# Bias rows made first, stored once, copied 128 times in DRAM and read in shifted rows from ScalarE's queue

## The chip, the cores and the metric

The kernel runs on one core of a Trainium2 chip. A core has TensorE (PE, matmuls into PSUM banks), VectorE (DVE), ScalarE (ACT), GpSimd (POOL) and SyncE (SP), which issues DMAs; ScalarE can issue DMAs from a queue of its own too. 16 DMA engines move the data. The metric is device time in microseconds (us) for one execution, the median of the runs.

## What is computed

Two blocks of two layers each, over 512 tokens of width 1024. The change touches the first block only. There each layer projects the tokens with one wide matrix, runs three attentions and projects back:

```python
def hybrid_layer(x, w_in, w_out, ...):
    h = rms_norm(x, g_pre)
    a_q, a_kv, a_g, b_cq, b_ckv, b_kr, c_q, c_kv, z = split_cols(h @ w_in)
    o_a = nsa_attention(..., rel_bias[:NSA_HEADS])        # 4 heads: compressed, selected, window
    ...
    o_b = causal_block_attention(...)                     # 4 heads, no relative bias
    o_c = banded_attention(..., SWA_WINDOW, rel_bias[NSA_HEADS:], sinks)   # 8 heads, window 128
    mixed = concatenate([o_a, o_b, o_c]) * silu(z)
    return x + rms_norm(mixed @ w_out, g_post)
```

Attentions a and c add to each logit a bias that depends on the head and on the distance of query and key alone: `bias_heads[:, t5_bucket(dist)]`, a table of 32 buckets for each of the 12 heads. In the second block (pooling, a recurrence and two feed-forward layers per layer) nothing changes.

## The kernel before

All weights are streamed from DRAM in tiles of 128 x 1024 (512 KB). `fetch_first` (L338) issues the load of tile n from SyncE into one of four raw buffers. VectorE casts it to a rounded part (`one_hi`, L172) and subtracts to get the rest (`one_lo`, L174), into one of two slots; PE multiplies both with the rounded activations and the rounded part with the rest of the activations, 24 matmuls per tile. A raw buffer is free when its tile is split (`w_split`), so SyncE's program in `attend` is a row of waits and fetches, tile n after the split of tile n - 4.

The first layer's 24 input tiles run in order 0 to 23. Tiles 0 and 1 are multiplied together while x arrives (`rows_arriving`, L219 to L222), later ones by `weight_tile` (L449, L453, L456). After tile 3 PE sums the squares of x (L1048); ScalarE then makes 1/rms by Ln and Exp (L702, L705), and only then VectorE evicts the finished banks into `proj` (L789, L791). Six banks are free at the start, so tile 6 is the first that needs an eviction, and VectorE's program evicts tiles 0 to 3 before it casts the tile 6. At tile 10 VectorE uses `s1`, a set of small weights (L875, `nsink`); after tile 18 PE uses `w1`. ScalarE issues both loads (L699, L700) after its passes over x. Behind the input tiles come 48 attention pairs, in the order NSA (24 pairs, tiles 0 and 1 of the output), MLA (8), sliding window (16).

The relative bias is made on the chip. `distance_rows` multiplies the table `rel` (32 x 12) with a one-hot matrix `hot` of the distances (L559: 4 heads x 1024 distances in two matmuls, L562: 8 heads x 384), `mask_rows` adds a mask (L569, L572), and the result is `vec` on partitions 0 to 3 and `near` on partitions 0 to 7. For the attention, row p of a bias tile must be the head's row shifted by p. This is done through DRAM: `store_bias` writes each head's row 128 times (`far_bias` 4 x 128 x 1024, 2.10 MB; `near_bias` 8 x 128 x 384, 1.57 MB), and `read_bias` reads with a partition step one element shorter than the row, into `biasA` and `biasC`.

In this order: PE does `distance_rows` between tile 1 and tile 2 (it waits for five small loads, `k1` among them, which SyncE issues after x and two weight tiles); VectorE does `mask_rows` at i = 1; SyncE does `store_bias` after fetching tile 7 and `read_bias` after fetching tile 11. VectorE waits for `read_a` and `read_c` before the first attention pair and before the first sliding-window pair.

Of the kernel before, what the change touches and what calls it, by code (L numbers as in the profile page):

```python
# [27 lines left out]
P = 128  # L28
# [348 lines left out]
TURN_LAG, WEIGH_LAG = 3, 4  # L377
N_NSA, N_MLA = 24, 8
SPLIT_AT = (17, 20)
# [4 lines left out]
Y_BANKS = (0, 4, 1, 2, 6, 7, 3, 5)  # L384
XSUM_BANK = 3
Y_KEPT = 2

# [72 lines left out]
class First:  # L460


    def __init__(self, kit, ctx):
# [19 lines left out]
        with ExitStack() as early:  # L483
# [20 lines left out]
        self.start = kit.sems("start", ("gains_in", "x_in0", "x_in1", "x_in2", "x_in3", "loaded", "vec_mm", "vec_made",  # L504
                                        "stored", "read_a", "read_c", "set"))
        self.s = [kit.sems(f"first{l}", FIRST_SEMS) for l in range(DEPTH)]
# [3 lines left out]
def start_engines(kit, first):  # L510

    d, bank, st, s = kit.d, kit.bank, kit.stream, first.start

    def sync(sp):
        sp.dma_start(kit.gains[:], d["gains"]).then_inc(s["gains_in"], 16)
        for i in range(4):
            sp.dma_start(kit.x[:, 2 * i:2 * i + 2, :], d["x"][:, 2 * i:2 * i + 2, :]).then_inc(s[f"x_in{i}"], 16)
            if i < 2:
                fetch_first(sp, st, i)
        for dst, src in ((first.rel, "rel"), (first.hot, "hot"), (first.msk, "msk"), (first.msk_near, "msk_near"),  # L520
                         (kit.k1, "k1")):
# [24 lines left out]
    def vector(v):  # L546
        v.sem_inc(st.w_split, RAW_RING)
        v.memset(kit.eps[:, 0:1], NORM_EPS).then_inc(s["set"], 1)
        v.memset(kit.eps[:, 1:2], LN_EPS / ALPHA ** 2).then_inc(s["set"], 1)
        v.memset(kit.ones[:], 1.0).then_inc(s["set"], 1)  # L550

    def tensor(pe):
        pe.sem_inc(st.mm_done, HL_RING)
        pe.wait_ge(s["set"], 3)

    def distance_rows(pe):
        pe.wait_ge(s["loaded"], 80)
        for i in range(2):
            pe.matmul(bank[(5, 3)[i]][0:A_HEADS, :], first.rel[:, 0:A_HEADS], first.hot[:, i * T:(i + 1) * T],  # L559
                      start=True, stop=True).then_inc(s["vec_mm"], 1)  # L560
        pe.wait_ge(s["vec_made"], 1)
        pe.matmul(bank[5][0:C_HEADS, 0:NEAR_W], first.rel[:, A_HEADS:], first.hot[:, 256:256 + NEAR_W],  # L562
                  start=True, stop=True).then_inc(s["vec_mm"], 1)

    def mask_rows(v):
        v.wait_ge(s["loaded"], 80)
# [5 lines left out]
        v.tensor_tensor(first.near[:], bank[5][0:C_HEADS, 0:NEAR_W], first.msk_near[:], ALU.add  # L572
                        ).then_inc(s["vec_made"], 1)

    return dict(sync=sync, store_bias=store_bias, read_bias=read_bias, scalar=scalar, vector=vector, tensor=tensor,
                distance_rows=distance_rows, mask_rows=mask_rows)


def attend(kit, first, l, begin):
# [26 lines left out]
    turn_bank = [(3, 6)[g % 2] for g in range(len(groups))]  # L606
    out_bank = {t: (4, 7)[i % 2] for i, t in enumerate(TILES)}

# [70 lines left out]
    def sync(sp):  # L679
        for n in range(max(n0, RAW_RING), n0 + st.per_layer):  # L680
            sp.wait_ge(st.w_split, n + 1)
            fetch_first(sp, st, n)
            if n == 7:
                begin["store_bias"](sp)
            if n == 11:
                begin["read_bias"](sp)

    def scalar(a):
# [63 lines left out]

        convert_at = {NU - 4: (0, 1), NU - 3: (2, 3), NU - 2: (4,), NU: (5,), NU + 1: (6,)}
        for j in range(NU + TURN_LAG):
            for i in here(j):
                u = pairs[i]
                w = u["width"]
                if u["kind"] == "swa":
                    a.wait_ge(s["sinks_in"], i + 1 - N_NSA - N_MLA)
                    w += 1  # L760
# [5 lines left out]
            for x in here(j - TURN_LAG):  # L766
                for g in groups_of[x]:
                    if not copied_by_v[g]:
# [4 lines left out]
                        a.activation(dst, src, ACT.Copy).then_inc(s["pt_by_a"], 1)  # L773
            for p in convert_at.get(j, ()):
                convert(p)
        convert(DC - 1)

    def vector(v):
# [27 lines left out]
        def step(j):  # L806
            for x in here(j - WEIGH_LAG - 1):
                if x == NU - 1 or pairs[x + 1]["tile"] != pairs[x]["tile"]:
                    tile = pairs[x]["tile"]
                    v.wait_ge(s["pv_mm"], x + 1)  # L810
# [46 lines left out]
        for i in range(N_IN):  # L857
            if i < N_IN - HL_RING:
                split(i + HL_RING)
            if i == 1:  # L860
                if l == 0:
                    begin["mask_rows"](v)
                for c in range(1, DC):
# [9 lines left out]
            if i == 10:  # L873
# [5 lines left out]
                if l == 0:  # L879
                    v.wait_ge(start["stored"], 32)  # L880
                v.tensor_tensor(rot_k[:, 0, :], proj[64:96, C_KR, :], cos, ALU.mult).then_inc(s["rot_made"], 1)
                v.tensor_tensor(rot_k[:, 1, :], proj[96:128, C_KR, :], sin, ALU.mult).then_inc(s["rot_made"], 1)
# [51 lines left out]
        v.wait_ge(s["z_made"], DC)  # L934
        v.wait_ge(start["read_a"], 16)
        for j in range(NU + WEIGH_LAG + 1):
            if j == N_NSA + N_MLA:
                v.wait_ge(start["read_c"], 16)
# [4 lines left out]
    def tensor(pe):  # L943
# [33 lines left out]
        def weigh(x):  # L977
# [3 lines left out]
            wait_copies(pe, groups_of[x][-1])  # L981
            order = TILES.index(tile)
            if order >= 2:
                pe.wait_ge(s["mixed"], order - 1)
            for y in range(u["m"]):
# [6 lines left out]
        def step(j):  # L992
            for i in here(j):
                if i >= 2:
                    pe.wait_ge(s["logits"], 2 * (i - 1))
                if i == 0:
                    pe.wait_ge(s["kc_made"], 2)
                if i == N_NSA:
                    pe.wait_ge(s["qk_made"], 2 * B_HEADS)
                    pe.wait_ge(s["uk_kept"], B_HEADS)  # L1000
                for hh in range(2):
                    logits(i, hh)
# [26 lines left out]
        if before:  # L1029
# [3 lines left out]
                      lambda k: pe.wait_ge(s["xhi_made"], k + 1), lambda k: pe.wait_ge(s["xlo_made"], k + 1))  # L1033
        if l == 0:
            begin["distance_rows"](pe)
        for i in range(2, N_IN):
# [5 lines left out]
            if i == 3:  # L1042
                if l == 0:
                    pe.wait_ge(start["vec_made"], 3)
                if before:
# [3 lines left out]
                          ).then_inc(s["xsq_summed"], 1)  # L1049
            if i == 12:  # L1050
                pe.wait_ge(s["taken"], C_KR + 1)
                for n in range(NT):
# [61 lines left out]
    def gpsimd(g):  # L1114
# [4 lines left out]
        for i in range(NU):  # L1119
            g.wait_ge(s["inv_made"], i + 1)  # L1120
            if i == 0:
                g.wait_ge(s["gates"], 4)
# [1339 lines left out]
```

## Time and profile before

| | us |
|---|---|
| median of 3 runs (lowest to highest) | 2673.74 (2669.78 to 2679.16) |
| profiled execution | 2676.89 |
| its span, first to last instruction | 2674.8 |
| busy in it: PE / DVE / ACT / POOL | 2472.3 / 1294.3 / 661.5 / 654.8 |
| mean granted TensorE clock | 0.962 |

The profile is one execution. A timeline row gives the start, the time taken, the engine (SPq and ACTq are DMA issues), the line, output and input, and in brackets the idle time before it and what ended that. Neighbours of one kind are merged into a row with their count. A row of windows gives busy times in a stretch, the granted clock (1.00 is full), the share of 16 DMA engines that was busy and the rate. Wait rows name who waited for whom.

### The profile page before, as it was taken

The page shows a single profiled execution, that of the slowest core. Times are in us where ns is not written, and L with a number is a line of the kernel's source. Part 1 is how long each engine was busy: PE and PEld are TensorE (multiplying, and loading weights), DVE is VectorE, ACT ScalarE, POOL GpSimd, SP SyncE. Part 2 cuts the span into 40 slices and gives each one's busy share as a digit, 9 for nine tenths or more (in the row PEclk, how much of TensorE's full clock was granted, in tenths as well). Part 3 has the DMA queues.
Part 4 walks back from the last instruction along what each step waited for, and adds up shares of the span by engine and source line. Part 5 has one row for each costly group of instructions (what it writes and reads, how often), then busy time and mean ns, then how long its engine had stood idle before and what let it go on. Part 6 is the DMA issues. An engine that isn't in the chain of part 4 may idle for free. (4 is left out here: it accounts for less than half of the span.)

```text
span 2674.8 us, 35071 instructions
## 1 busy us (share of the span) xinstructions
PE 2472.3 (92%) x13238; PEld 1985.8 (74%) x13238; DVE 1294.3 (48%) x1920; ACT 661.5 (25%) x1329; POOL 654.8 (24%) x510
## 2 busy tenths in 40 slices
PE   7089999999789999999899999899999998999997
PEld 5066677866668888788688888788888787788886
DVE  4045656557453334586643334433343776533344
ACT  3001643037121110253321110311100643311101
POOL 1000561016333331200333321233311101433311
PEclk9589999999989999998999999999999998999999
DMA  5341013200033332221223232223322221223322
GB/s 166 56 139 47 17 48 126 86 25 17 16 117 98 98 109 93 71 98 41 79 87 101 94 117 92 64 94 98 107 98 83 95 65 56 79 95 101 111 99 78
DMA packets 58641, 224.79 MB, mean 84 GB/s; under 512 B 6392, under 2 KB 8576, under 8 KB 58276
## 3 DMA queue, kind: packets, MB, share of 16 engines
q1 hardware_dynamic: 57380, 215.49, 25.3%
q10 hardware_dynamic: 1152, 7.78, 0.8%
q8 instruction: 77, 1.26, 0.2%
q14 instruction: 32, 0.26, 0.0%
HBM read 217.47 MB, written 5.77 MB: 83 GB/s over the span
## 5 line engine op out<-in xcount | busy, mean ns | idle before, releaser
L172 DVE CAST two_hi<-two_raw 128x1024 fp32r<-128x1024 f32 (+1 forms) x292 | 219.8, 753 | 908.0 <-PE bank L241 896.5
L234 PE MATMUL bank<-xh,two_hi 128*128 128x512 f32 x1728 | 429.6, 391 | 0.0
L241 PE MATMUL bank<-xl,two_hi 128*128 128x512 f32 x1728 | 427.5, 389 | 0.0
L237 PE MATMUL bank<-xh,two_lo 128*128 128x512 f32 x1728 | 426.9, 389 | 0.0
L174 DVE TENSOR_TENSOR two_lo<-two_raw,two_hi 128x1024 fp32r<-128x1024 f32 (+1 forms) x292 | 401.0, 1373 | 10.0
L237 PEld LDWEIGHTS bank<-xh,two_lo 128*128 128x128 f32 x1728 | 324.3, 188 | 67.5
L241 PEld LDWEIGHTS bank<-xl,two_hi 128*128 128x128 f32 x1728 | 324.3, 188 | 67.4
L234 PEld LDWEIGHTS bank<-xh,two_hi 128*128 128x128 f32 x1728 | 323.0, 188 | 68.2 <-issue 1.1
L1579 POOL TENSOR_TENSOR up_hm<-up_sg,up_hm 128x512 f32<-128x512 f32 x88 | 197.6, 2245 | 556.4 <-ACT up_hm L1561 556.4
L449 PE MATMUL bank<-xh,one_hi 128*128 128x512 f32 x448 | 122.5, 418 | 81.0 <-DVE one_hi L172 81.0
L234 PE MATMUL bank<-hh,two_hi 128*128 128x512 f32 x704 | 171.8, 392 | 0.0
L172 DVE CAST one_hi<-one_raw 128x1024 fp32r<-128x1024 f32 x64 | 45.5, 710 | 260.6 <-PE bank L456 134.8
L241 PE MATMUL bank<-hl,two_hi 128*128 128x512 f32 x704 | 171.4, 390 | 0.0
L237 PE MATMUL bank<-hh,two_lo 128*128 128x512 f32 x704 | 170.0, 389 | 0.0
L449 PEld LDWEIGHTS bank<-xh,one_hi 128*128 128x128 f32 x448 | 88.0, 198 | 104.8 <-issue 86.0
L1561 ACT ACTIVATE up_hm<-bank 128x512 f32<-128x512 f32 x88 | 52.9, 601 | 416.5 <-PE bank L241 413.7
L665 POOL TENSOR_SCALAR lg_ring<-lg_ring,inv,gate 128x31 f32<-128x31 f32 (+4 forms) x80 | 45.0, 570 | 450.6 <-DVE inv L799 450.3
L234 PEld LDWEIGHTS bank<-hh,two_hi 128*128 128x128 f32 x704 | 132.1, 188 | 29.3 <-issue 1.9
L237 PEld LDWEIGHTS bank<-hh,two_lo 128*128 128x128 f32 x704 | 132.1, 188 | 27.5
L241 PEld LDWEIGHTS bank<-hl,two_hi 128*128 128x128 f32 x704 | 132.2, 188 | 27.3
L1582 POOL TENSOR_TENSOR hl<-up_hm,hh 128x512 f32 x88 | 115.1, 1308 | 83.7 <-ACT hh L1563 83.7
L453 PE MATMUL bank<-xh,one_lo 128*128 128x512 f32 x448 | 112.7, 394 | 0.0
(289 smaller groups left out, 2923.2 us busy)
## 6 DMA issues: line engine op xcount, KB each, us to landing
two_raw<-in_up SPq DMA_DIRECT2D x180, 512.0 KB, 3.4
two_raw<-in_down SPq DMA_DIRECT2D x64, 704.0 KB, 4.0
one_raw<-in_w_in SPq DMA_DIRECT2D x48, 512.0 KB, 3.5
two_raw<-in_w_in SPq DMA_DIRECT2D x40, 512.0 KB, 3.4
one_raw<-in_w_out SPq DMA_DIRECT2D x16, 512.0 KB, 3.4
two_raw<-in_w_out SPq DMA_DIRECT2D x16, 512.0 KB, 4.1
w<-in_w ACTq DMA_DIRECT2D x2, 2048.0 KB, 11.6
x<-in_x SPq DMA_DIRECT2D x4, 512.0 KB, 6.9
```

What stands on the lines that cost most here:

```text
L172: v.tensor_copy(st.hi[:, h, 0:w], st.raw[:, r, 0:w]).then_inc(st.hi_made, 1)
L174: v.tensor_tensor(st.lo[:, h, 0:w], st.raw[:, r, 0:w], st.hi[:, h, 0:w].bitcast(F32), ALU.subtract).then_inc(st.w_split, 1)
L234: pe.matmul(out[:], st.hi[:, slot, k * P:(k + 1) * P], xh[:, h * kp + k, :], start=h == 0 and k == 0, stop=False)
L237: pe.matmul(out[:], st.lo[:, slot, k * P:(k + 1) * P], xh[:, h * kp + k, :], start=False, stop=False)
L241: mm = pe.matmul(out[:], st.hi[:, slot, k * P:(k + 1) * P], xl[:, h * kp + k, :], start=False, stop=h == pieces - 1 and k == kp - 1)
L449: pe.matmul(out[:], st.hi[:, slot, w * P:(w + 1) * P], xh[:, k, :], start=k == 0, stop=False)
L453: pe.matmul(out[:], st.lo[:, slot, w * P:(w + 1) * P], xh[:, k, :], start=False, stop=False)
L665: return eng.tensor_scalar(row, row, inv[:, i, hh:hh + 1], gate[:, u["n"], b:b + 1], ALU.mult, ALU.mult)
L1561: a.activation(hm[:, f, :], bank[1][:], ACT.Copy).then_inc(s["out_taken"], 1)
L1579: g.tensor_tensor(hm[:, f, :], sg[:, f, :], hm[:, f, :], ALU.mult).then_inc(s["h_made"], 1)
L1582: g.tensor_tensor(hl[:, at, :].rearrange("p o t -> p (o t)"), hm[:, f, :], hh[:, at, :].rearrange("p o t -> p (o t)").bitcast(F32), ALU.su ...
```

## The change

The row matmuls and the masked adds are done before the first weight tile is split; their inputs `rel`, `hot`, `msk`, `msk_near` are loaded first, and the near matmul uses bank 7, so that it need not wait for bank 5. SyncE stores the rows once (`far_row`, `near_row`, 28 KB). ScalarE copies them 128 times from DRAM to DRAM behind its passes over x, ahead of the loads of s1 and w1, and issues the shifted reads after the last of its eight Silu passes, behind a wait for the copies. `k1` has its own semaphore and is loaded after the row stores. Some constants of the attention's order are written as expressions.

```diff
     def sync(sp):
+        for dst, src in ((first.rel, "rel"), (first.hot, "hot"), (first.msk, "msk"), (first.msk_near, "msk_near")):
+            sp.dma_start(dst[:], d[src]).then_inc(s["loaded"], 16)
         sp.dma_start(kit.gains[:], d["gains"]).then_inc(s["gains_in"], 16)
         for i in range(4):
             sp.dma_start(kit.x[:, 2 * i:2 * i + 2, :], d["x"][:, 2 * i:2 * i + 2, :]).then_inc(s[f"x_in{i}"], 16)
             if i < 2:
                 fetch_first(sp, st, i)
-        for dst, src in ((first.rel, "rel"), (first.hot, "hot"), (first.msk, "msk"), (first.msk_near, "msk_near"),
-                         (kit.k1, "k1")):
-            sp.dma_start(dst[:], d[src]).then_inc(s["loaded"], 16)
         for n in (2, 3):
             fetch_first(sp, st, n)
-
-    def store_bias(sp):
         sp.wait_ge(s["vec_made"], 3)
-        sp.dma_start(d["far"], first.vec[0:A_HEADS].unsqueeze(1).to_broadcast([A_HEADS, P, 2 * T])
-                     ).then_inc(s["stored"], 16)
-        sp.dma_start(d["near"], first.near[:].unsqueeze(1).to_broadcast([C_HEADS, P, NEAR_W])).then_inc(s["stored"], 16)
-
-    def read_bias(sp):
-
-        sp.wait_ge(s["stored"], 32)
-        for dst, name, sem, heads, w, n in ((kit.biasC, "near", "read_c", C_HEADS, NEAR_W, 256),
-                                            (kit.biasA, "far", "read_a", A_HEADS, 2 * T, BIAS_W)):
+        sp.dma_start(d["far_row"], first.vec[:]).then_inc(s["stored"], 16)
+        sp.dma_start(d["near_row"], first.near[:]).then_inc(s["stored"], 16)
+        sp.dma_start(kit.k1[:], d["k1"]).then_inc(s["k1_in"], 16)
+
+    spread = (("near", "read_c", kit.biasC, C_HEADS, NEAR_W, 256), ("far", "read_a", kit.biasA, A_HEADS, 2 * T, BIAS_W))
+
+    def copy_bias(a):
+
+        a.wait_ge(s["stored"], 32)
+        for name, _, _, heads, w, _ in spread:
+            row = d[f"{name}_row"]
+            a.dma_start(d[name], bass.AP(row.tensor, row.offset, [[w, heads], [0, P], [1, w]])).then_inc(s["copied"], 16)
+
+    def read_bias(a):
+
+        a.wait_ge(s["copied"], 32)
+        for name, sem, dst, heads, w, n in spread:
             src = d[name]
-            sp.dma_start(dst[:], bass.AP(src.tensor, src.offset + P - 1, [[w - 1, P], [w * P, heads], [1, n]])
-                         ).then_inc(s[sem], 16)
+            a.dma_start(dst[:], bass.AP(src.tensor, src.offset + P - 1, [[w - 1, P], [w * P, heads], [1, n]])
+                        ).then_inc(s[sem], 16)
...
         v.memset(kit.ones[:], 1.0).then_inc(s["set"], 1)
+        mask_rows(v)
 
     def tensor(pe):
         pe.sem_inc(st.mm_done, HL_RING)
         pe.wait_ge(s["set"], 3)
-
-    def distance_rows(pe):
-        pe.wait_ge(s["loaded"], 80)
+        pe.wait_ge(s["loaded"], 64)
         for i in range(2):
             pe.matmul(bank[(5, 3)[i]][0:A_HEADS, :], first.rel[:, 0:A_HEADS], first.hot[:, i * T:(i + 1) * T],
                       start=True, stop=True).then_inc(s["vec_mm"], 1)
-        pe.wait_ge(s["vec_made"], 1)
-        pe.matmul(bank[5][0:C_HEADS, 0:NEAR_W], first.rel[:, A_HEADS:], first.hot[:, 256:256 + NEAR_W],
+        pe.matmul(bank[7][0:C_HEADS, 0:NEAR_W], first.rel[:, A_HEADS:], first.hot[:, 256:256 + NEAR_W],
                   start=True, stop=True).then_inc(s["vec_mm"], 1)
...
             fetch_first(sp, st, n)
-            if n == 7:
-                begin["store_bias"](sp)
-            if n == 11:
-                begin["read_bias"](sp)
...
             a.activation(xsq[:, c, :], kit.x[:, c, :], ACT.Square).then_inc(s["xsq_made"], 1)
+        if l == 0:
+            begin["copy_bias"](a)
         a.dma_start(s1[:], d["s1"][l]).then_inc(s["s1_in"], 16)
         a.dma_start(w1[:], d["w1"][l]).then_inc(s["w1_in"], 16)
...
             a.activation(proj[:, C_Z + c, :], proj[:, C_Z + c, :], ACT.Silu).then_inc(s["z_made"], 1)
+            if l == 0 and c == DC - 1:
+                begin["read_bias"](a)
...
-        convert_at = {NU - 4: (0, 1), NU - 3: (2, 3), NU - 2: (4,), NU: (5,), NU + 1: (6,)}
+        convert_at = {}
+        for p in range(DC - 1):
+            at = max(NU - L_RING + p // 2 + TURN_LAG + 1, last_of[TILES[p]] + WEIGH_LAG + 2, *convert_at)
+            convert_at.setdefault(at, []).append(p)
...
+    for kind, heads, w in (("far", A_HEADS, 2 * T), ("near", C_HEADS, NEAR_W)):
+        dram[f"{kind}_row"] = nc.dram_tensor(f"{kind}_bias_row", (heads, w), F32, kind="Internal").ap()
```

## Rows read from the trace of the kernel before

**Rows 1.** The page's slices: busy tenths of PE and of the DMA engines.
```profile
PE   7089999999789999999899999899999998999997
...
DMA  5341013200033332221223232223322221223322
```
**Rows 2.** Waits from 0 to 160 us: who waited for whom, us in total, times, longest.
```profile
DVE one_hi L172 <- DMA one_raw<-in_w_in: 93.8, 2, 88.4
...
PE bank L449 <- DVE one_hi L172: 81.0, 1, 81.0
```
**Rows 3.** Timeline of SyncE's DMA issues around the stores and reads of the bias.
```profile
30.82 34.25 SPq L530 DMA_DIRECT2D near_bias<-near  x1
...
65.11 56.72 SPq L345 DMA_DIRECT2D one_raw<-in_w_in  x1
...
143.66 0.39 SPq L538 DMA_DIRECT2D biasC<-near_bias  x1
```
**Rows 4.** Timeline of PE: first matmuls of tile 7, tile 8, tile 9 and tile 10.
```profile
59.18 1.98 PE L449 MATMUL bank<-xh,one_hi 128*128 128x512 f32 x8
...
145.76 3.75 PE L449 MATMUL bank<-xh,one_hi 128*128 128x512 f32 x8 [80.98 <-DVE one_hi L172]
...
153.09 1.98 PE L449 MATMUL bank<-xh,one_hi 128*128 128x512 f32 x8
...
158.53 1.98 PE L449 MATMUL bank<-xh,one_hi 128*128 128x512 f32 x8
```
**Rows 5.** Windows; the last three columns are granted clock, DMA share and GB/s.
```profile
17.50:20.00 2.50, 2.50 (x13) 2.06 (x12) 0.00 (x0) 2.46 (x5) 2.09 (x2) 1.00 1.02 415
...
30.00:33.00 3.00, 3.00 (x9) 2.38 (x8) 2.64 (x4) 0.00 (x0) 0.00 (x0) 0.52 0.48 157
...
36.00:64.00 28.00, 28.00 (x123) 22.79 (x123) 11.37 (x14) 6.06 (x9) 0.00 (x0) 1.00 0.24 26
66.00:96.00 30.00, 0.00 (x0) 0.00 (x0) 0.00 (x0) 0.00 (x0) 0.00 (x0) 0.53 0.46 51
```
**Rows 6.** Timeline of PE and DVE: row matmuls, masked adds, tile 2, start of tile 3.
```profile
25.53 1.88 PE L559 MATMUL bank<-hot,rel 32*4 32x512 f32 x4
...
27.85 1.27 DVE L569 TENSOR_TENSOR vec<-bank,msk 4x512 f32<-4x512 f32 x2
...
28.58 0.81 PE L562 MATMUL bank<-hot,rel 32*8 32x384 f32 x2 [1.18 <-DVE vec L569]
29.31 3.14 PE L449 MATMUL bank<-xh,one_hi 128*128 128x512 f32 x8
...
36.51 1.98 PE L449 MATMUL bank<-xh,one_hi 128*128 128x512 f32 x8
```
**Rows 7.** Timeline of the start: issues of x, rel and k1, first cast, PE's run.
```profile
1.22 0.41 SPq L517 DMA_DIRECT2D x<-in_x  x1
...
4.33 0.74 SPq L522 DMA_DIRECT2D rel<-in_rel  x1
...
5.49 0.72 ACT L695 ACTIVATE xh<-x,gains 128x512 fp32r<-128x512 f32 x1 [3.46 <-DMA x<-in_x]
...
6.41 0.36 SPq L522 DMA_DIRECT2D k<-in_k  x1
6.67 0.69 DVE L172 CAST one_hi<-one_raw 128x1024 fp32r<-128x1024 f32 x1 [5.49 <-DMA one_raw<-in_w_in]
...
13.51 0.80 PE L219 MATMUL bank<-xh,one_hi 128*128 128x512 f32 x1 [2.66 <-DVE one_lo L174]
```
**Rows 8.** Timeline: the norm's Ln on ScalarE, and VectorE's first use of s1.
```profile
43.01 0.69 ACT L702 ACTIVATE xrstd<-bank,eps 128x512 f32<-128x512 f32 x1 [23.05 <-PE bank L1048]
...
166.72 0.16 DVE L875 TENSOR_SCALAR nsink<-s 128x8 f32<-128x8 f32 x1
```
**Rows 9.** Timeline: one conversion of xh; and a window inside the last stores, columns as in 5.
```profile
360.71 0.62 ACT L751 ACTIVATE xh<-proj 128x512 fp32r<-128x512 f32 x1
...
2666.50:2668.00 1.50, 0.00 (x0) 0.00 (x0) 1.46 (x3) 0.72 (x1) 0.00 (x0) 0.50 0.69 281
```

More of the change, by code:

```diff
@@ L385 @@
 XSUM_BANK = 3
+OUT_BANKS = (4, 7, 4, 7, 4, 7, 4, 7)
 Y_KEPT = 2
@@ L504, in __init__ @@
         self.start = kit.sems("start", ("gains_in", "x_in0", "x_in1", "x_in2", "x_in3", "loaded", "vec_mm", "vec_made",
-                                        "stored", "read_a", "read_c", "set"))
+                                        "k1_in", "stored", "copied", "read_a", "read_c", "set"))
         self.s = [kit.sems(f"first{l}", FIRST_SEMS) for l in range(DEPTH)]
@@ L571, in mask_rows @@
         v.wait_ge(s["vec_mm"], 3)
-        v.tensor_tensor(first.near[:], bank[5][0:C_HEADS, 0:NEAR_W], first.msk_near[:], ALU.add
+        v.tensor_tensor(first.near[:], bank[7][0:C_HEADS, 0:NEAR_W], first.msk_near[:], ALU.add
                         ).then_inc(s["vec_made"], 1)
-    return dict(sync=sync, store_bias=store_bias, read_bias=read_bias, scalar=scalar, vector=vector, tensor=tensor,
-                distance_rows=distance_rows, mask_rows=mask_rows)
+    return dict(sync=sync, copy_bias=copy_bias, read_bias=read_bias, scalar=scalar, vector=vector, tensor=tensor)
 def attend(kit, first, l, begin):
@@ L606, in attend @@
     turn_bank = [(3, 6)[g % 2] for g in range(len(groups))]
-    out_bank = {t: (4, 7)[i % 2] for i, t in enumerate(TILES)}
+    out_bank = {t: OUT_BANKS[i] for i, t in enumerate(TILES)}
+    last_of = {u["tile"]: i for i, u in enumerate(pairs)}
+    first_of = {kind: min(i for i, u in enumerate(pairs) if u["kind"] == kind) for kind in ("cmp", "mla", "swa")}
+    n_swa = [sum(u["kind"] == "swa" for u in pairs[:i + 1]) for i in range(NU)]
+    assert list(TILES) == sorted(TILES, key=last_of.get)
     def here(j):
@@ L758, in scalar @@
                 if u["kind"] == "swa":
-                    a.wait_ge(s["sinks_in"], i + 1 - N_NSA - N_MLA)
+                    a.wait_ge(s["sinks_in"], n_swa[i])
                     w += 1
@@ L773, in scalar @@
                         a.activation(dst, src, ACT.Copy).then_inc(s["pt_by_a"], 1)
-            for p in convert_at.get(j, ()):
+            for p in convert_at.pop(j, ()):
+                convert(p)
+        for late in convert_at.values():
+            for p in late:
                 convert(p)
@@ L807, in step @@
             for x in here(j - WEIGH_LAG - 1):
-                if x == NU - 1 or pairs[x + 1]["tile"] != pairs[x]["tile"]:
-                    tile = pairs[x]["tile"]
+                tile = pairs[x]["tile"]
+                if x == last_of[tile]:
                     v.wait_ge(s["pv_mm"], x + 1)
@@ L860, in vector @@
             if i == 1:
-                if l == 0:
-                    begin["mask_rows"](v)
                 for c in range(1, DC):
@@ L880, in vector @@
                     v.wait_ge(start["stored"], 32)
+                    v.wait_ge(start["k1_in"], 16)
                 v.tensor_tensor(rot_k[:, 0, :], proj[64:96, C_KR, :], cos, ALU.mult).then_inc(s["rot_made"], 1)
@@ L934, in vector @@
         v.wait_ge(s["z_made"], DC)
-        v.wait_ge(start["read_a"], 16)
         for j in range(NU + WEIGH_LAG + 1):
-            if j == N_NSA + N_MLA:
+            if j == first_of["cmp"]:
+                v.wait_ge(start["read_a"], 16)
+            if j == first_of["swa"]:
                 v.wait_ge(start["read_c"], 16)
@@ L981, in weigh @@
             wait_copies(pe, groups_of[x][-1])
-            order = TILES.index(tile)
-            if order >= 2:
-                pe.wait_ge(s["mixed"], order - 1)
+            ahead = [p for p in range(TILES.index(tile)) if OUT_BANKS[p] == out_bank[tile]]
+            if ahead:
+                pe.wait_ge(s["mixed"], ahead[-1] + 1)
             for y in range(u["m"]):
@@ L995, in step @@
                     pe.wait_ge(s["logits"], 2 * (i - 1))
-                if i == 0:
-                    pe.wait_ge(s["kc_made"], 2)
-                if i == N_NSA:
+                if i == first_of["mla"]:
                     pe.wait_ge(s["qk_made"], 2 * B_HEADS)
                     pe.wait_ge(s["uk_kept"], B_HEADS)
+                if i == first_of["cmp"]:
+                    pe.wait_ge(s["kc_made"], 2)
                 for hh in range(2):
@@ L1033, in tensor @@
                       lambda k: pe.wait_ge(s["xhi_made"], k + 1), lambda k: pe.wait_ge(s["xlo_made"], k + 1))
-        if l == 0:
-            begin["distance_rows"](pe)
         for i in range(2, N_IN):
@@ L1050, in tensor @@
             if i == 12:
+                if l == 0:
+                    pe.wait_ge(start["k1_in"], 16)
                 pe.wait_ge(s["taken"], C_KR + 1)
@@ L1120, in gpsimd @@
             g.wait_ge(s["inv_made"], i + 1)
-            if i == 0:
+            if i == first_of["cmp"]:
                 g.wait_ge(s["gates"], 4)
```

3 lines of the change are left out of this document (1 added, 2 removed).

## The prediction

> **What bounds the kernel now.** I read the slices of the page first: TensorE (PE) is busy in nine tenths or more of nearly every slice, except the second, where it does nothing, and the DMA line falls to 1 to 3 tenths around it [rows 1]. The kernel is bound by TensorE, so the second slice (67 to 134 us) is pure loss. The list of waits names it: PE waits 81.0 us once for the first cast (L172) of a weight tile, and that cast waits 88.4 us for its DMA [rows 2]. The timeline of SyncE's queue says why. The near store's issue, right behind the far one's, begins at 30.82 and takes 34.25 us, and the next weight fetch's issue takes 56.72 us; the reads of the bias follow at 143.66, when the near store has landed [rows 3]. PE ran to 64.8 us on the eight weight tiles fetched ahead of the stores, and started tile 8 at 145.76 [rows 4].
>
> How fast the stores go is in the windows. While only the far store moves (36 to 64 us) the DMA share is 0.24, which is four of 16 engines, at 26 GB/s in all; from 66 to 96 us it is 0.46 at 51 GB/s, twice each. When ordinary loads run, 16 engines move 415 GB/s, 26 GB/s each [rows 5]. So one DMA engine carries one head's copies, and four engines that read partitions 0 to 3 together get what one engine gets in a load: 6.5 GB/s each. The far store alone (2.10 MB) needs 81 us at 26 GB/s; near heads 0 to 3 wait behind it on the same engines. All weight fetches use all 16 engines in queue order, so they wait too. The Trainium skill gives the rule for it ("SBUF — State Buffer", Door 1: The DMA port swizzle): partitions 0 to 3 share one of 16 ports. The trace agrees, with its 26 GB/s for four engines and 51 for eight.
>
> **The change, part by part.** All terms are against the profiled execution, 2676.9 us (span 2674.8).
>
> 1. The hole. The bulk copies leave SyncE's queue, whose stores are now 28 KB instead of 3.67 MB. Weight fetches then find their queue free, as between tiles 2 and 7. A tile takes 5.44 us on PE (158.53 less 153.09), so tile 9 would begin at 59.18 + 10.88 = 70.1 where it began at 153.09 [rows 4]: 83.0 us. That is the wait of 81.0 plus 1.9 us by which tile 8 ran long (7.33 us). The granted clock had fallen to 0.50 while PE idled [rows 5]. What is late next is worked out in 4 and 5.
>
> 2. The row matmuls. Before, they stood between tiles 1 and 2: PE began them at 25.53, began tile 2 at 29.31, and tile 2 took until 36.51, 7.20 us in place of 5.44, with the granted clock at 0.52 from 30 to 33 us [rows 6, 5]. Without them tile 2 follows at once: 3.8 + 1.7 = 5.5 us gained.
>
> 3. The start. SyncE now issues four small loads ahead of the gains and x: 6.41 less 4.33 = 2.1 us of issue, by which x and weight tile 0 (cast at 6.67) come later, about 8.8 [rows 7]. VectorE (DVE) now does the three masked adds (two take 1.27 us, [rows 6]) before its first split, and waits for PE's row matmuls. The loads are issued by 2.8 us and the first of the kind needs about 2 us to land, an estimate from x, which ACT could use 4.3 us after its issue with half a megabyte in it. Then 4.8 us; the far matmuls take 1.9 us at full clock, perhaps 3.5 on a cold one; a third of 0.8 to 1.3, a last add: 9 to 10.5 us. So the splits begin 2.1 to 3.8 us later than at 6.67 and with them PE's run from 13.51. I take 3.7, near the upper end, since PE has not run by then: lost. Terms 2 and 3 give -1.8. SyncE itself waits in front of the row stores until 10.5, and behind them are k1 and fetch 4. Fetch 4 needs the first split (about 14 us now), so nothing waits for that.
>
> 4. ScalarE's queue. The two copies are issued there, behind a wait for the row stores (they queue behind about 4.3 MB of loads at 0.4 MB/us, so they land at about 17 to 18; copies flow from 19). Behind that wait stand s1, w1, and then Ln and Exp of the norm, without which DVE can evict nothing. An issue can block: the near store's returned when 34 of the far store's 81 us were gone [rows 3], that is with some 75 of 128 pieces left on each engine. So the issue of s1 returns when the last 60% of the far copy remain. The Ln began at 43.01 [rows 8], now 41.2. DVE's order puts four evictions (2.5 us) and the cast of tile 6 (0.7) behind Ln and Exp (1.4), and PE wants tile 6 at 59.18 - 5.44 - 1.8 = 51.9: ScalarE may be late until 47.3 without loss.
> What does a copy from DRAM to DRAM cost? No row shows one. From below: an engine reads DRAM at 26 GB/s [rows 5] and writes DRAM at 25.5 (the last stores, 281 GB/s on a share of 0.69, [rows 9]). If both sides overlap it is 0.16 us for 4 KB; if they follow each other, 12.8 GB/s and 0.32 us. From above: 6.5 GB/s as in the old store, though here no SBUF partition is read. Far has 128 pieces of 4 KB on each of 4 engines, near 128 of 1.5 KB on each of 8 (taking the same split by heads). Overlapped: near 7.7, far 20.5 us. Serial: near 15.4, far 41 us; s1's issue returns after 15.4 + 0.41 x 41 = 32 us, at 51, and at 59 if the fetches of 5 to 9 and k1 (8 us on each engine) fit into no gap. Late by 4 to 12 us; I take serial, and 8 us: the engine reads and writes the same memory, and a source row of 4 KB is read 128 times over. The Trainium skill ("DMA: Bandwidth & Descriptors", Latency and other measured facts) has 207 to 214 GB/s each way for copies between HBM tensors, 13 GB/s an engine; by it the sum would be the serial one. No run here shows it yet.
>
> 5. s1, w1 and the reads. s1 is needed at 166.72 [rows 8], now 82 (90 with the 8 us of term 4). The far copy ends at 19 + 56 = 75, at most 92 with all fetches serial; s1 lands some 3 us later. Covered or nearly: up to 5 us in the range. w1 is needed by PE after tile 18, past 120. The reads of biasC and biasA hold ScalarE until the copies are done; behind it is work of tile 12 and later (from about 90), and biasA is wanted only when the attention begins, past 170. Nothing.
>
> 6. The rest of the diff writes constants as expressions of the pair list. With this order the values are the same, but for one: converting p = 5 (0.62 us, [rows 9]) comes two pairs earlier, in both layers. 0, between -0.6 and +0.6 each.
>
> Sum: -83.0 - 1.8 + 8 = -76.8, so 2600 us against the profiled 2676.9. The median of the runs is 3.1 us under that execution: 2597.
>
> The rule of the skill that speaks against the change is in the same page ("DMA: Bandwidth & Descriptors", Issuing engines are not separate DMA queues): work issued by ScalarE runs on the same 16 DMA engines, so that another queue only saves issue time. The trace before shows only one queue busy in the hole. By that rule the transfer itself gains nothing from the move; my gain comes from order within a queue and from the source.
>
> **The rivals.**
> A. Copies overlap, 26 GB/s an engine: s1's issue returns at 19 + 16 + 8 = 43, before 47.3. No stall: 2676.9 - 84.8 = 2592, median 2589. For it: both sides alone run at that speed. Against it: one row read over and over, and reads and writes in one memory.
> B. The copy is as slow as the store was, 6.5 GB/s an engine: near 30, far 81 us; s1's issue returns at 19 + 30 + 33 = 82, late by 35; s1 lands at about 138, where 82 + 35 = 117 was wanted, 20 more: -85 + 55, 2647, median 2644. This is also the case in which the change doesn't do what it says. For it: the same piece sizes and four engines. Against: eight engines gave 51 GB/s on other partitions, so partitions, not pieces, set the pace.
> C. Slower than before: the copy from DRAM doesn't split by heads but goes on one engine. 3.67 MB at 26 GB/s is 141 us, s1's issue returns at about 19 + 60 + 70 = 149, late by 102 against 84.8 gained: +17, 2694, median 2691; at the serial price +150. At the serial price it decides below three engines. For it: no row shows a split of a copy without partitions; against: its outer dimension is the heads as before.
> D. One descriptor generator serves both queues, so SyncE's fetches 6 and 7 (at 30 us) wait behind the copies until 51 to 59. Tile 6 then begins at about 60 instead of 51.9, beside the stall of term 4 and not on top: 2 us more than the forecast. It lies within it.
>
> **How the numbers follow.** Serial copies (with D) 0.47; A 0.30; between serial and B, or B itself, 0.17; C 0.03; others, mostly a few us of the start, 0.03. The forecast is 2597. Bounds: 2583 (A with a start that costs 2 and not 3.7, and a few us of unseen gain) to 2628 (an engine at about 8 GB/s: near 25, far 66, s1's issue back at 71, late by 24, and s1 then some 6 late). That leaves out B proper and C. Under 0.3% (8 us) this kernel's runs can't tell from no change. Faster 0.95, same 0.01, slower 0.04 (C, and something like it).
>
> **What would show it.** No wait of cast L172 on its DMA over 5 us, PE in the second slice at 9 tenths, tile 2 right behind tile 1 at full clock; DMA share near 0.25 to 0.5 at 50 to 200 GB/s beside the fetches from 19 us on; the issue of s1 on ScalarE's queue some 30 to 40 us long and Ln at 50 to 58 instead of 41. If Ln is at 41, A was right; if DVE waits at nsink for s1, B. Wrong altogether if the fetches of SyncE wait on the shared DMA engines behind the copies, tile after tile, longer than 5.44 us each: that would be a new hole between 50 and 90 us.

## The result and the profile after

| | before | after |
|---|---|---|
| median of 4 runs (lowest to highest), us | 2676.45 (2669.78 to 2680.52) | 2591.00 (2590.79 to 2591.41) |
| profiled execution / its span, us | 2676.89 / 2674.8 | 2590.79 / 2588.9 |
| mean granted clock | 0.962 | 0.977 |

The ratio is 0.9683, 95% interval 0.9661 to 0.9705: 3.2% faster, some 85 us. The forecast was 2597, the range 2583 to 2628. (The kernel before has one run more here than ahead of the prediction, where its median was 2673.74.)

The page's slices of the changed kernel, the rows that answer to [rows 1]. The second slice is full now:

```profile
PE   8999999998799999998999999999999999999997
...
DMA  6300132000333322211223332222321312222332
```

The waits from 0 to 100 us. The 88 us of [rows 2] are gone. What VectorE's cast waits for is PE: 12.2 us once, for tiles 0 and 1, and after that pieces of at most 3.5 us, as it should be where PE is the bound:

```profile
DVE one_hi L172 <- PE bank L456: 25.6, 10, 3.5
ACT xrstd L706 <- PE bank L1058: 20.3, 1, 20.3
```

The timeline of the changed kernel in order of time, from several engines: masked adds and the first cast, PE's run, the copies on ScalarE's queue, tiles 2 and 3, a fetch of SyncE, the issues of s1 and w1, and the norm's Ln (compare [rows 3, 6, 7, 8]).

```profile
6.14 0.68 DVE L572 TENSOR_TENSOR vec<-bank,msk 4x512 f32<-4x512 f32 x1 [4.97 <-PE bank L563]
...
9.53 0.67 DVE L172 CAST one_hi<-one_raw 128x1024 fp32r<-128x1024 f32 x1
...
16.36 0.80 PE L219 MATMUL bank<-xh,one_hi 128*128 128x512 f32 x1 [2.67 <-DVE one_lo L174]
16.44 1.24 ACTq L536 DMA_DIRECT2D near_bias<-near_bias_row  x1
...
17.72 4.94 ACTq L536 DMA_DIRECT2D far_bias<-far_bias_row  x1
...
22.69 16.18 ACTq L703 DMA_DIRECT2D s<-in_s  x1
...
29.80 1.98 PE L449 MATMUL bank<-xh,one_hi 128*128 128x512 f32 x8
...
30.46 0.33 SPq L345 DMA_DIRECT2D one_raw<-in_w_in  x1
...
35.24 1.98 PE L449 MATMUL bank<-xh,one_hi 128*128 128x512 f32 x8
...
38.90 1.21 ACTq L704 DMA_DIRECT2D w<-in_w  x1
41.74 0.69 ACT L706 ACTIVATE xrstd<-bank,eps 128x512 f32<-128x512 f32 x1 [20.33 <-PE bank L1058]
```

In this execution Ln waits for PE and for nothing else. PE runs without a wait from 16.4 to 100 us; tile 9 begins here, where [rows 4] have 153.09:

```profile
68.78 1.98 PE L449 MATMUL bank<-xh,one_hi 128*128 128x512 f32 x8
```

And the windows, with the columns of [rows 5] (the last three: granted clock, DMA share, GB/s). From 20 to 27 us the near copy moves on half of the engines, at 28 us the far one on a quarter, and at 36 us four engines are shared about evenly by the two queues, the far copy on ScalarE's (13.4% of the 16 engines' time) and weight fetches on SyncE's (12.6%):

```profile
20.00:27.00 7.00, 7.00 (x27) 5.67 (x26) 0.00 (x0) 1.40 (x3) 1.18 (x1) 1.00 0.53 199
28.00:30.00 2.00, 2.00 (x10) 1.68 (x9) 1.49 (x2) 0.00 (x0) 0.00 (x0) 1.00 0.26 105
36.00:38.00 2.00, 2.00 (x11) 1.65 (x10) 1.79 (x4) 0.00 (x0) 0.00 (x0) 1.00 0.26 107
```

That is 24 to 26 GB/s for each engine, four times the pace of the old store (0.24 and 26 GB/s in [rows 5]), on the same number of engines.

### The profile page after: what moved, and what is told of

It reads as the page before. It is cut to its first block and busy times, and to the rows that moved or that the text cites. A ratio compares the mean times of both kernels' runs of the same rounds, so it can differ in the third digit from the quotient of the medians.

```text
span 2588.9 us, 35076 instructions
## 1 busy us (share of the span) xinstructions
PE 2472.0 (95%) x13238; PEld 1983.8 (77%) x13238; DVE 1294.7 (50%) x1920; ACT 662.0 (26%) x1329; POOL 655.2 (25%) x510
## 5 line engine op out<-in xcount | busy, mean ns | idle before, releaser
L449 PE MATMUL bank<-xh,one_hi 128*128 128x512 f32 x448 | 116.0, 401 | 0.0
L1575 ACT ACTIVATE hh<-up_hm 128x512 f32 x88 | 55.6, 632 | 215.9 <-POOL up_hm L1591 215.9
```

The source lines that it names most:

```text
L449: pe.matmul(out[:], st.hi[:, slot, w * P:(w + 1) * P], xh[:, k, :], start=k == 0, stop=False)
L1575: a.activation(hh[:, bass.ds(j * 2 + f, 1), :].rearrange("p o t -> p (o t)"), hm[:, f, :], ACT.Copy).then_inc(s["hhi_made"], 1)
```

## The experiments

All times are medians. The changed kernel was timed twice more beside the later ones: 2589.83 (2587.74 to 2595.11) and 2590.98 (2587.30 to 2595.25), where its first four runs lay within 0.6. So kernels of about 2590 have a spread of some 8 us within their runs, and differences of 2 or 3 us between two of them aren't decided by the times.

### What made the old store slow: source or queue

Four corners were wanted: SBUF or DRAM as the source, SyncE's or ScalarE's queue. Two are the kernels before and after, which differ in more than that: the rows are made first in the one after. The third is the changed kernel, reading SBUF from ScalarE's queue:

```diff
-        for name, _, _, heads, w, _ in spread:
-            row = d[f"{name}_row"]
-            a.dma_start(d[name], bass.AP(row.tensor, row.offset, [[w, heads], [0, P], [1, w]])).then_inc(s["copied"], 16)
+        for name, src, heads, w in (("near", first.near, C_HEADS, NEAR_W), ("far", first.vec, A_HEADS, 2 * T)):
+            a.dma_start(d[name], src[0:heads].unsqueeze(1).to_broadcast([heads, P, w])).then_inc(s["copied"], 16)
```

> The changed kernel, but ScalarE's two bulk transfers read the rows from SBUF (128 times each, as the kernel before did) and not from DRAM. Theory SOURCE (the SBUF partitions read set the pace, 6.5 GB/s an engine): the near transfer takes about 31 us, the far one 81; s1's issue returns at about 81 us instead of 38.9, so Ln begins at 82, 35 us later than PE can bear, and s1 lands at about 133 where 117 would be wanted: 2591 + 35 + 16 = 2642 us, up to 2660 if the weight fetches crawl on the shared engines 0 to 3. Theory QUEUE (the gain came from taking the bulk off SyncE's queue): within 10 us of 2591.

Measured: 2644.75 us (2641.47 to 2647.18), ratio 0.9884 (0.9860 to 0.9908). Its timeline of ScalarE and its queue:

```profile
18.00 9.78 ACTq L535 DMA_DIRECT2D far_bias<-vec  x1
27.82 55.91 ACTq L702 DMA_DIRECT2D s<-in_s  x1
83.76 4.96 ACTq L703 DMA_DIRECT2D w<-in_w  x1
88.77 0.69 ACT L705 ACTIVATE xrstd<-bank,eps 128x512 f32<-128x512 f32 x1 [67.11 <-issue]
```

PE's wait in the list of waits up to 160 us (sum, count, longest):

```profile
PE bank L449 <- DVE one_hi L172: 49.3, 3, 41.0
```

The last of its three pieces in the timeline, with what VectorE waited for just before:

```profile
137.71 0.17 DVE L884 TENSOR_SCALAR nsink<-s 128x8 f32<-128x8 f32 x1 [7.31 <-DMA s<-in_s]
...
142.71 3.75 PE L449 MATMUL bank<-xh,one_hi 128*128 128x512 f32 x8 [7.95 <-DVE one_hi L172]
```

And a window, with the columns of [rows 5]:

```profile
64.00:70.00 6.00, 0.00 (x0) 0.00 (x0) 0.00 (x0) 0.00 (x0) 0.00 (x0) 0.50 0.24 25
```

The rate is the old one, 25 GB/s on four engines. ScalarE sat in the issue of s1 for 55.9 us, and PE waited 41.0 us for the evictions behind it. Later it waited 7.95 us for the cast of tile 13, which stands behind `nsink` in VectorE's program, and `nsink` waited for s1. The third piece, 0.4 us, is the only one that a weight tile's fetch caused. This is rival B, and its time (2644) fits in part by luck: it had 35 us for Ln and 20 for s1, where 41.0, 8.0 and some 4 us at the lower clock were measured (tile 6 took 7.26 us instead of 5.44, tile 13 8.18 instead of 5.60). Moving the bulk to the other queue, with the rows made first, saves 35 of 85 us and makes a new wait.

The fourth corner is the kernel before with DRAM as the source, in SyncE's queue at the old place:

```diff
...
-        sp.dma_start(d["far"], first.vec[0:A_HEADS].unsqueeze(1).to_broadcast([A_HEADS, P, 2 * T])
-                     ).then_inc(s["stored"], 16)
-        sp.dma_start(d["near"], first.near[:].unsqueeze(1).to_broadcast([C_HEADS, P, NEAR_W])).then_inc(s["stored"], 16)
+        sp.dma_start(d["far_row"], first.vec[:]).then_inc(s["rows"], 16)
+        sp.dma_start(d["near_row"], first.near[:]).then_inc(s["rows"], 16)
+        sp.wait_ge(s["rows"], 32)
+        for name, heads, w in (("far", A_HEADS, 2 * T), ("near", C_HEADS, NEAR_W)):
+            row = d[f"{name}_row"]
+            sp.dma_start(d[name], bass.AP(row.tensor, row.offset, [[w, heads], [0, P], [1, w]])).then_inc(s["stored"], 16)
```

> The kernel before with one edit: SyncE stores each row once, waits for that, and then copies from DRAM 128 times, all in its own queue at the place of the old store. Theory SOURCE: far 20 us and near 8 us on a few engines from about 33 us, done by about 62, fetch 8 lands by about 64, when PE wants it: no hole, 2676 - 83 = 2593 us (up to 2603). Theory QUEUE: the fetches still stand behind the bulk in one queue, so most of the hole stays: 2650 us or more.

Measured: 2586.07 us (2585.36 to 2591.69), ratio 0.9668 (0.9642 to 0.9694). The queue theory is out. In its trace the far copy runs at 104 GB/s on a share of 0.25, the near store's issue, 34.25 us in [rows 3], takes 7.78:

```profile
33.13 0.72 SPq L533 DMA_DIRECT2D far_bias<-far_bias_row  x1
33.90 7.78 SPq L533 DMA_DIRECT2D near_bias<-near_bias_row  x1
```

Of the hole this is left on PE:

```profile
65.71 2.08 PE L449 MATMUL bank<-xh,one_hi 128*128 128x512 f32 x8 [1.95 <-DVE one_hi L172]
```

So the change of source alone gives the whole gain that the times resolve. It was timed a second time beside the changed kernel:

> The kernel before with the DRAM source alone, copies on SyncE's queue, timed a second time beside the changed kernel. If the source is the whole gain: equal to the changed kernel within 3 us. If the rest of the change (rows first, ScalarE's queue) is worth something by itself, the changed kernel is faster by more than 3 us. From the first time it may be up to 5 us faster than the changed kernel: its PE begins 3 us earlier, pays 3.8 for the row matmuls and 2 for a rest of the hole.

Measured: 2593.62 us (2584.73 to 2595.62) against 2590.98. The two aren't told apart by this; the first time it had stood 5 us below the changed kernel's 2591. Rows made first and the change of queue are worth nothing by themselves that these runs resolve.

### Why that source was slow

The kernel before once more, still from SBUF and from SyncE's queue, with each head's row on a partition of its own four (0, 4, 8 and so on; the tables are made four times as tall, each row four times):

```diff
...
-        sp.dma_start(d["far"], first.vec[0:A_HEADS].unsqueeze(1).to_broadcast([A_HEADS, P, 2 * T])
+        sp.dma_start(d["far"], first.vec[0:4 * A_HEADS:4].unsqueeze(1).to_broadcast([A_HEADS, P, 2 * T])
...
-        sp.dma_start(d["near"], first.near[:].unsqueeze(1).to_broadcast([C_HEADS, P, NEAR_W])).then_inc(s["stored"], 16)
+        sp.dma_start(d["near"], first.near[0:4 * C_HEADS:4].unsqueeze(1).to_broadcast([C_HEADS, P, NEAR_W])).then_inc(s["stored"], 16)
...
-            pe.matmul(bank[(5, 3)[i]][0:A_HEADS, :], first.rel[:, 0:A_HEADS], first.hot[:, i * T:(i + 1) * T],
+            pe.matmul(bank[(5, 3)[i]][0:4 * A_HEADS, :], first.rel[:, 0:4 * A_HEADS], first.hot[:, i * T:(i + 1) * T],
...
```

> The kernel before with one edit: the head rows lie on partitions 0, 4, 8, ... instead of 0, 1, 2, ... (rel, msk, vec and near are four times as tall, each row four times), and the bulk store reads one partition of each four. Still from SBUF, on SyncE's queue, at the old place. If it is the four neighbouring partitions that share 26 GB/s: four engines move about 104 GB/s in the far store, the hole is gone, 2593 us. If a read of one SBUF partition over and over is slow by itself (6.5 GB/s an engine): the hole stays, 2676 us.

Measured: 2588.96 us (2585.41 to 2591.24), ratio 0.9668 (0.9644 to 0.9692). In the window of its far store four engines move 108 GB/s out of SBUF:

```profile
36.00:40.00 4.00, 4.00 (x17) 3.27 (x16) 1.55 (x3) 0.00 (x0) 0.00 (x0) 0.91 0.27 108
```

Reading one partition 128 times isn't slow; four engines reading partitions 0 to 3 are, together. This is the rule of the Trainium skill named in the prediction ("SBUF — State Buffer", Door 1: The DMA port swizzle): partitions 0 to 3 lie behind one port, and 0, 4, 8 and 12 behind four. The trace agrees: 26 GB/s from four partitions of one port, 108 from four ports.

### What a blocked issue costs

The changed kernel with the far copy issued a second time:

```diff
...
+        row = d["far_row"]
+        a.dma_start(d["spare"], bass.AP(row.tensor, row.offset, [[2 * T, A_HEADS], [0, P], [1, 2 * T]])).then_inc(s["copied"], 16)
...
```

> The changed kernel with the far copy issued a second time, into a spare tensor, ahead of s1. It tests the price of a blocked issue and the latest time for Ln. s1's issue should return some 20 us later, at about 59 us, and Ln begin at about 60 instead of 41.7. PE wants tile 6 at 52.5 and Ln must begin by 47.9 for that, so 12.5 us are lost: 2603 us. If the extra copy only uses idle engines and no issue waits for it: 2591 us. If a late s1 or slow fetches count too: above 2610 us.

Measured: 2610.12 us (2607.77 to 2613.10), 19 more than the changed kernel. ScalarE's queue and the first matmuls of tile 6:

```profile
22.36 16.22 ACTq L538 DMA_DIRECT2D spare_bias<-far_bias_row  x1
38.62 22.16 ACTq L705 DMA_DIRECT2D s<-in_s  x1
60.82 1.20 ACTq L706 DMA_DIRECT2D w<-in_w  x1
62.07 0.69 ACT L708 ACTIVATE xrstd<-bank,eps 128x512 f32<-128x512 f32 x1 [40.52 <-issue]
...
66.75 3.75 PE L449 MATMUL bank<-xh,one_hi 128*128 128x512 f32 x8 [15.53 <-DVE one_hi L172]
```

The chain is as worked out: 4.7 us from Ln to the matmuls of tile 6. The further copy held the issue of s1 by its own length, 22 us. PE waited 15.5 and not 12.5: Ln came 2 us later than I had set, and PE was 1.4 us further on in this execution (tile 6 due at 51.05, not 52.46), which adds to the wait and not to the time. The tile after the wait took 7.37 us (66.75 to 74.12) and not 5.44, the granted clock having gone to 0.50: 1.9 us, which I had left out. So tile 7 begins 16.2 us later than in the changed kernel (74.12, there 57.90), of 18.1 by which the two spans differ; another 1.5 are gone by the start of the attention (194.55, there 176.87), at a dip of the clock that comes by chance (see the sum of what was measured, below).

The changed kernel with the rows made late, between tiles 1 and 2 as before, copies on ScalarE's queue:

```diff
-        for dst, src in ((first.rel, "rel"), (first.hot, "hot"), (first.msk, "msk"), (first.msk_near, "msk_near")):
-            sp.dma_start(dst[:], d[src]).then_inc(s["loaded"], 16)
         sp.dma_start(kit.gains[:], d["gains"]).then_inc(s["gains_in"], 16)
...
+            if n == 7:
+                begin["store_rows"](sp)
...
+        if l == 0:
+            begin["distance_rows"](pe)
         for i in range(2, N_IN):
```

> The changed kernel with the first part undone: the four small loads are issued after x, the row matmuls stand between tiles 1 and 2 again and the masked adds behind the fourth split; the copies stay on ScalarE's queue and now start at about 32 us. Theory ISSUE BLOCKS: s1's issue returns 22 us after the copies start, w1's a little later, so Ln begins at about 56 instead of 41.7; PE can bear 48 to 49 here, 7 us are lost, plus 1.3 for the row matmuls' place: 2599 us. Rival (early rows matter only for the row matmuls' place and the clock): 2592 us.

Measured: 2601.01 us (2598.32 to 2605.54), ratio 0.9722 (0.9706 to 0.9738), against 2589.83 for the changed kernel beside it. The intervals lie apart.

```profile
35.65 17.01 ACTq L709 DMA_DIRECT2D s<-in_s  x1
...
53.94 0.69 ACT L712 ACTIVATE xrstd<-bank,eps 128x512 f32<-128x512 f32 x1 [34.19 <-issue]
...
58.62 3.75 PE L449 MATMUL bank<-xh,one_hi 128*128 128x512 f32 x8 [7.49 <-DVE one_hi L172]
```

So making the rows first is not idle: on ScalarE's queue it keeps the issue of s1 from holding Ln. 7.5 us of wait were expected as 7. The tile behind the wait took 8.35 us (58.62 to 66.97) instead of 5.44, so the clock took 2.9 more, which again wasn't in the expectation: 10.4 of the 11.2. It pays for the choice of that queue, no more.

### Can the rest be had

Copies over 16 engines (the 128 repeats outermost in both patterns):

```diff
-            a.dma_start(d[name], bass.AP(row.tensor, row.offset, [[w, heads], [0, P], [1, w]])).then_inc(s["copied"], 16)
+            dst = d[name]
+            a.dma_start(bass.AP(dst.tensor, dst.offset, [[w, P], [P * w, heads], [1, w]]),
+                        bass.AP(row.tensor, row.offset, [[0, P], [w, heads], [1, w]])).then_inc(s["copied"], 16)
```

> The changed kernel with the 128 copies as the outermost dimension of the two copies, so that 16 engines and not 8 and 4 should share each: the DMA share goes to 1.0 at some 400 GB/s from 18 us, all done in about 9 us, s1's issue returns before 30 us. The time stays within 1 us of 2591, since ScalarE was free 5 us before it had to be. If the copies beside the weight fetches cost anything hidden, up to 3 us are gained.

Measured: 2590.01 us (2587.27 to 2598.60). w1's issue is over at 20.9 us instead of 40.1. From 22 to 24 us ScalarE's queue alone moves, nearly all of it the near copy's 1.5 KB pieces:

```profile
22.00:24.00 2.00, 2.00 (x11) 1.65 (x10) 0.00 (x0) 0.00 (x0) 0.00 (x0) 1.00 0.89 307
```

That is 21.5 GB/s an engine, where the same pieces ran at 23.5 on eight engines (199 GB/s on a share of 0.53); in the 2 us behind it the rate was 233 on 0.77, 19. The expectation had some 400 GB/s and all done in 9 us; the far copy landed at 34.9. The time doesn't move: all of it lay beside other work already.

The cheaper start: the small loads from ScalarE's queue, the masked adds behind the first two splits.

```diff
...
     def sync(sp):
-        for dst, src in ((first.rel, "rel"), (first.hot, "hot"), (first.msk, "msk"), (first.msk_near, "msk_near")):
-            sp.dma_start(dst[:], d[src]).then_inc(s["loaded"], 16)
...
     def scalar(a):
+        for dst, src in ((first.rel, "rel"), (first.hot, "hot"), (first.msk, "msk"), (first.msk_near, "msk_near")):
+            a.dma_start(dst[:], d[src]).then_inc(s["loaded"], 16)
...
-        mask_rows(v)
...
             for i in range(HL_RING):
                 split(i)
+            begin["mask_rows"](v)
```

> The changed kernel with a cheaper start: ScalarE issues the four small loads at once, so that SyncE's gains, x and weight tile 0 come as early as in the kernel before, and VectorE splits the first two tiles before the masked adds. PE does the row matmuls in its idle time before tile 0. The run of PE should begin at about 13.5 us instead of 16.4, and the copies at about 18: 2588 us. If the start is not what sets tile 0 (the arrival of x does): 2591 us. If Ln comes too late because the copies start later: above 2591.

Measured: 2590.86 us (2588.00 to 2594.38) against 2589.83. In the trace tile 2 begins at 27.68 where the changed kernel beside it has 29.64, but the changed kernel's own executions differ here (29.80, 29.64, 28.52), and of the 2.0 us 1.7 are lost again at tile 19, which takes 9.1 us here and 7.5 there (127.79 to 136.93, 129.75 to 137.24). The times don't show a gain. PE's run began at 15.09, not 13.5: the first cast was at 8.23, 1.6 later than in [rows 7], probably because the loads from the second queue land among x's; no run shows that apart. This run came nearest to the edge: Ln at 45.01 with the issue of s1 as what held it, and PE wanted it by 45.7 (tile 6 at 50.35, less 4.7).

The 16 engines once more, now in the kernel before with DRAM as the source (SyncE's queue, the old place):

```diff
-            sp.dma_start(d[name], bass.AP(row.tensor, row.offset, [[w, heads], [0, P], [1, w]])).then_inc(s["stored"], 16)
+            dst = d[name]
+            sp.dma_start(bass.AP(dst.tensor, dst.offset, [[w, P], [P * w, heads], [1, w]]),
+                         bass.AP(row.tensor, row.offset, [[0, P], [w, heads], [1, w]])).then_inc(s["stored"], 16)
```

> The same, with the 128 copies outermost, so that 16 engines share them: done in about 9 us at some 400 GB/s, before fetch 8 is issued. The 2 us that PE waited before tile 8 go: 2 us less than the kernel before it in this call, if the spread lets it be seen; in the trace the wait of PE on the cast of tile 8 is gone.

Measured: 2588.25 us (2587.26 to 2593.76) against 2590.98 for the changed kernel and 2593.62 for the same with few engines. There is no wait before tile 8 in the trace, as expected (62.40, 67.84, 73.28: three tiles at 5.44). But there is none either in the trace with few engines beside it (63.33, 68.77, 74.20), where PE was later by itself. What the 16 engines changed is seen on VectorE, at the cast of tile 8, first with few engines, then with 16:

```profile
67.42 0.69 DVE L172 CAST one_hi<-one_raw 128x1024 fp32r<-128x1024 f32 x1 [6.71 <-DMA one_raw<-in_w_in]
...
62.67 0.69 DVE L172 CAST one_hi<-one_raw 128x1024 fp32r<-128x1024 f32 x1 [2.88 <-PE bank L456]
```

The tile had come in time for PE in both; in the first run of the DRAM source it hadn't, by 1.95 us.

And the cheaper start together with copies over 16 engines:

```diff
-            a.dma_start(d[name], bass.AP(row.tensor, row.offset, [[w, heads], [0, P], [1, w]])).then_inc(s["copied"], 16)
+            dst = d[name]
+            a.dma_start(bass.AP(dst.tensor, dst.offset, [[w, P], [P * w, heads], [1, w]]),
+                        bass.AP(row.tensor, row.offset, [[0, P], [w, heads], [1, w]])).then_inc(s["copied"], 16)
...
```

> The changed kernel with the cheaper start (small loads issued by ScalarE, splits ahead of the masked adds) and copies over 16 engines. Tile 2 begins 2 us earlier than in the changed kernel and ScalarE is free by 25 us: 2588 us, 2 less than the changed kernel in this call.

Measured: 2589.98 us (2588.59 to 2590.28); tile 2 begins at 27.48, in the changed kernel beside it at 28.52: 1 us and not the 2 expected. None of these is faster than the changed kernel by more than the spread. From 16.4 us to the attention, at 177, PE waits for 2.7 us in all in the changed kernel; the rest there is its own work. Not tried: the loads of s1 and w1 ahead of the copies. In the kernel before each was issued in under 0.5 us, at 13.4 and 13.8, and only the copies' own issues would then stand ahead of Ln.

## Why the prediction was right, point by point

The hole (term 1) came out to the tenth: tile 9 moved from 153.09 to 68.78, 84.3 us, and tile 3 from 36.51 to 35.24, 1.3, so 83.0 lie between them, as forecast. The reading behind it was right too: the second experiment on the source and the one on the partitions show that the pace of the read, not its place in a queue, made the hole. There I stressed the wrong half: term 1 gave the gain to the copies' leaving SyncE's queue, and the part on a rule of the Trainium skill said that it came from order and source together. The runs give it to the source; the other queue, with the rows made first, gives 35 us of 85.

The row matmuls (term 2): from the end of tiles 0 and 1 to tile 3 it was 36.51 - 25.53 = 11.0 us and is 35.24 - 29.80 = 5.4. Forecast 5.5, measured 5.5.

The start (term 3): PE's run began at 16.36 instead of 13.51, 2.9 later, where I took 3.7. But tiles 0 and 1 were done 4.3 us later (29.80 instead of 25.53): PE's matmuls stood 0.43 us apart and not 0.23 until 22.5 us, 6.1 us of its run, and before only until 16.6, 3.1 us. That wasn't in the sum. Net of 2 and 3 a gain of 1.3, forecast 1.8.

ScalarE's queue (term 4) is the term that was mis-sized. I took a copy from DRAM to DRAM as a read followed by a write, 12.8 GB/s an engine, and 8 us for a late Ln. The engine read and wrote at once, 24 to 26 GB/s; s1's issue returned at 38.9 and Ln wasn't held: 0. This was rival A, with 2589 as its median and 0.30 as its chance. The reason that I gave, one source row read 128 times over in the memory that is also written, had no effect that the windows show. The figure of the Trainium skill that the prediction names ("DMA: Bandwidth & Descriptors", Latency and other measured facts), 207 to 214 GB/s each way, is for tiles of 128 partitions by 16 KiB between HBM tensors; it isn't borne out for these rows: 307 GB/s in a window of the run with 16 engines. The mechanism was right: the issue does block, and wherever it bites PE's wait is near the one worked out (41.0 us for 35 with the SBUF source, 15.5 for 12.5 with the second far copy, 7.5 for 7 with the late rows), while the slow tile behind each wait was left out. There are 6 us between 41.7 and the latest time that PE can bear, 47.8 (tile 6 at 52.46 less 4.7). It isn't always so wide: in a later execution of the changed kernel the issue of w1 ended at 41.27 and Ln began at 41.32, 0.9 us after the sums it needs were done, still 5 us early enough.

s1, w1 and the reads (term 5): s1 landed at 58 us and was used at 82.4; the reads of the bias were issued at 66.2 without a wait for the copies. Nothing, as forecast. The converted p = 5 (term 6): from the first attention pair to the end the spans are 2411.6 us before and 2411.7 after. So nothing is seen either, though an effect of 0.6 us could hide: the granted clock at the start of the attention was 0.98 before (265 to 280 us) and 0.70 after (180.7 to 195.7).

Rival D is refuted. While ScalarE was stuck in the issue of s1, from 22.69 to 38.90, SyncE issued a fetch at 30.46 in 0.33 us. Rival C, one engine, is excluded by the shares of 0.53 and 0.26. What the prediction says of fetches crawling behind copies on shared engines does happen (the window from 36 to 38 us), but it costs PE next to nothing: 0.4 us in the run with the SBUF source, 1.95 in the first run of the DRAM source in SyncE's own queue, none in the changed kernel.

Sum of what was measured: 84.3 to tile 9; 1.6 more until the attention starts (263.19 to 177.24); 0.0 after it. 85.9 of span. The 1.6 are chance: the granted clock before was 0.89 from 205 to 220 us, and tile 19 began with 3.59 us for eight matmuls, where the profiled execution of the changed kernel has 2.07 and a later one of the same kernel 3.66.

How near the forecast came is in part luck. The sum had 76.8 us where the span gives 85.9: 8 too little in term 4 and 1.6 for that chance, less 0.5 in terms 2 and 3. The step from the profiled execution to the median, 3.1 us, made up for a part of it, and with the fourth run of the kernel before that step is only 0.4. The range held the result since it had rival A in it; the case that had the largest chance, serial copies at 0.47, did not come. And its upper end doesn't follow from the working given for it: 84.8 less 24 and 6 is a gain of 54.8, which gives 2619 (2676.9 - 54.8 - 3.1), not 2628.

## What to carry to other kernels

When a DMA moves slowly, divide its rate by the engines that its share stands for, and compare with a load's: 26 GB/s for four engines together was the sign here that they drew from one port, and a move of the rows by four partitions, or one bounce through DRAM, was worth the whole 85 us, another queue 35. Before a bulk DMA goes to the queue of a computing engine, find the next issue behind it on that engine: here it blocked until much of the bulk had gone, and everything after it in the program waited along. This kernel had 6 us of room; with the rows made late it had none and 11 of the 85 us were lost. Double the transfer once to see where the room ends. And when a total agrees with a rival's price, check the parts: with the SBUF source it did, and two of its terms were off by 6 and 12 us.

## What was not expected of the hardware

- An engine copied from DRAM to DRAM as fast as it loads, 24 to 26 GB/s, with the same 4 KB read over and over; with all 16 at it and pieces of 1.5 KB, 19 to 21.5.
- A blocked issue held its own engine's program only: SyncE's took 0.33 us while ScalarE's took 16.2.
- After a wait of 7.5 to 81 us PE's next tile took 7.3 to 8.4 us instead of 5.4 to 5.6, with the granted clock at 0.50 at its start (of its levels 2.4 and 1.2 GHz, the lower): 1.8 to 2.9 us on top of each such wait. The longer waits didn't cost more: 7.33 us after 81.0, 7.26 after 41.0, 7.37 after 15.5, but 8.18 after 7.95 and 8.35 after 7.5.
- Where PE idled for only 1.2 us in the row matmuls, the clock fell in some executions and not in others: tile 2 took 7.2 us in [rows 6] and 5.6 in the first run of the DRAM source (29.92 to 35.49), but 8.0 when the same kernel was timed again (32.70 to 40.66). At tile 19 it fell in some without any wait before it. Each fall costs 1.5 to 2.5 us, a part of the spread of some 8 us. What decides it stays open.
